# Issuing the three late weight loads of an expert stage one by one

## The reference, cut to what matters

```python
hid = jax.nn.silu(jnp.einsum('nd,edf->nef', t, w_gate)) * jnp.einsum('nd,edf->nef', t, w_up)
hid = hid * combine[:, :, None].astype(hid.dtype)
y = jnp.einsum('nef,efd->nd', hid, w_down)
```

## Time and profile before

| | |
|---|---|
| median of 3 runs | 822.22 us (818.6 to 824.94) |
| the profiled execution's own time | 819.91 us |
| its span in the trace | 818.2 us |
| TensorE busy in the span | 765.6 us, 94% |
| VectorE, ScalarE busy | 605.0 us, 504.0 us |
| HBM read, written | 160.18 MB, 24.12 MB |

### The profile page before, as it was taken

One profiled execution on the slowest core, in us unless ns is written; L12 is line 12 of the kernel. 1 busy time (PEld: TensorE's weight loads), 2 busy tenths in 40 slices (PEclk: granted clock), 3 DMA queues, 4 the chain that ended last, 5 costly groups with the idle time before them and its releaser, 6 DMA issues.

```text
span 818.2 us, 11409 instructions
## 1 busy us (share of the span) xinstructions
PE 765.6 (94%) x4348; PEld 575.1 (70%) x4348; DVE 605.0 (74%) x838; ACT 504.0 (62%) x680; POOL 166.7 (20%) x157
## 2 busy tenths in 40 slices
PE   6999999799999899998998999999999899998993
PEld 4788876464789778777876554657579778876872
DVE  5898994985646798797896467667535789887992
ACT  6778505625315488696884137776735388786892
POOL 5220012400002213332120001043102222332113
PEclk9999999999999999999999999999999899999998
DMA  9975466214834599999987100142073599999953
GB/s 370 239 151 147 86 149 151 37 70 189 304 134 170 219 401 359 320 314 324 325 283 273 70 0 1 52 154 103 1 283 155 211 409 345 326 314 333 314 216 52
DMA packets 35403, 170.91 MB, mean 209 GB/s; under 512 B 7841, under 2 KB 10017, under 8 KB 19728
## 3 DMA queue, kind: packets, MB, share of 16 engines
q1 hardware_dynamic: 18432, 130.03, 41.8%
q0 software_dynamic: 15184, 34.56, 17.8%
q10 hardware_dynamic: 1728, 5.52, 1.9%
HBM read 160.18 MB, written 24.12 MB: 225 GB/s over the span
## 4 chain that ended last, share of the span: by engine, by line
PE 52%; DMA 18%; DVE 17%; ACT 7%; issue 2%; DVEq 1%; ACTq 0%; POOLq 0%; SPq 0%; POOL 0%
DMA ring<-stream 17%; PE PS L2188 9%; DVE w_lo L1117 8%; PE PS L2441 7%; PE PS L1925 7%; PE PS L2319 6%; PE PS L2344 3%; ACT w_hi L754 3%; PE PS L1976 3%; PE PS L2218 2%; PE PS L2476 2%; PE PS L2135 2%; PE PS L2499 1%; DMA arena<-rows 1%; DVE arena L1123 1%
## 5 line engine op out<-in xcount | busy, mean ns | idle before, releaser
L1117 DVE TENSOR_TENSOR w_lo<-ring,w_hi 128x2048 fp32r<-128x2048 f32 x92 | 209.9, 2288 | 42.3 <-ACT w_hi L754 36.1
L754 ACT ACTIVATE w_hi<-ring 128x2048 fp32r<-128x2048 f32 x86 | 164.6, 1916 | 44.0 <-DMA ring<-stream 39.9
L2319 PE MATMUL PS<-w_hi,left_hi 128*128 128x512 f32 x512 | 173.1, 404 | 7.5 <-DVE w_lo L1117 6.8
L2319 PEld LDWEIGHTS PS<-w_hi,left_hi 128*128 128x128 f32 x512 | 96.4, 189 | 30.2 <-issue 6.0
L2319 PE MATMUL PS<-w_lo,left_hi 128*128 128x512 f32 x256 | 99.0, 395 | 0.0
L2344 PE MATMUL PS<-w_hi,left_lo 128*128 128x512 f32 x256 | 85.0, 392 | 7.5 <-DVE left_lo L1117 5.5
L2441 PE MATMUL PS<-ring,hT 128*128 128x512 f32 (+1 forms) x192 | 73.5, 527 | 0.3 <-DVE hT L1117 0.3
L602 POOL DMA_INDIRECT arena<-rows x32 | 41.6, 1299 | 123.8 <-PE PS L2291 110.2
L2344 PEld LDWEIGHTS PS<-w_hi,left_lo 128*128 128x128 f32 x256 | 48.1, 188 | 19.4 <-DVE left_lo L1117 7.2
L2441 PEld LDWEIGHTS PS<-ring,hT 128*128 128x128 f32 x192 | 34.7, 190 | 28.8 <-issue 26.9
L2319 PEld LDWEIGHTS PS<-w_lo,left_hi 128*128 128x128 f32 x256 | 48.9, 191 | 8.6
(11 more groups left out here) (301 smaller groups left out, 1471.2 us busy)
## 6 DMA issues: line engine op xcount, KB each, us to landing
ring<-stream SPq DMA_DIRECT2D x110, 1024.0 KB, 15.9
arena<-stream SPq DMA_DIRECT2D x6, 1024.0 KB, 9.0
ring_split<-stream POOLq DMA_DIRECT2D x11, 512.0 KB, 5.5
rows<-arena POOLq DMA_DIRECT2D x8, 512.0 KB, 3.0
x<-stream SPq DMA_DIRECT2D x4, 1024.0 KB, 6.5
x<-x_in SPq DMA_DIRECT2D x4, 512.0 KB, 5.2
ring_split<-stream POOLq DMA_DIRECT2D x2, 1024.0 KB, 9.0
left_lo<-hT_hi POOLq DMA_DIRECT2D x2, 1024.0 KB, 11.5
```

What stands on the lines that cost most here:

```text
L754: act.activation(w_hi[pair], held_slot(layer, m), ACT.Copy).then_inc(w_hi_done, 1)
L1117: return V.tensor_tensor(out, a, b, op)
L2319: ins = mm(PS[:, gate_bank(e), :], a, b, start=k == 0 and t == 0, stop=k == KD - 1 and t == 2)
```

## The change

The three outside loads that were issued together ahead of ring piece 6 are issued one by one, each ahead of the ring piece that lies eleven pieces before it: 25 ahead of 14, 34 ahead of 23, 43 ahead of 32. The waits for the memory under them stay ahead of piece 6. Since they all count up one semaphore, each load now first waits until the outside loads before it have landed, and ScalarE's copy of an outside piece waits for the landing of that piece, not for all five (7 waits for the first two, like 16).

```diff
@@ -465,7 +465,9 @@
                         sp.wait_ge(first_row_in, 16 * (layer + 1))
                         for n in (NE * layer, NE * layer + 1):
                             sp.wait_ge(got_row[n % 3], fetched(n))
-                        for n in (2, 3, 4):
+                    for n in (2, 3, 4):
+                        if i == EXP0[layer] + AHEAD[n] - 11:
+                            sp.wait_ge(late_in, 16 * (len(AHEAD) * layer + n))
                             load_late(n, layer)
                 if i == QKV0 + 2:
                     sp.wait_ge(zeroed, 2)
@@ -741,7 +743,7 @@
 
                 i, pair = EXP0[layer] + m, expert_pair(layer, m)
                 if m in AHEAD:
-                    act.wait_ge(late_in, 16 * len(AHEAD) * (layer + 1))
+                    act.wait_ge(late_in, 16 * (len(AHEAD) * layer + max(AHEAD.index(m), 1) + 1))
                 else:
                     full, turn = filled(i)
                     act.wait_ge(full, 16 * turn)
```

## The result

The changed kernel is slower: 828.4 us in the median of 6 runs against 822.9 of the kernel before, ratio 1.0083 with an interval of 1.0056 to 1.0111. So the change costs 5.5 us by the medians and 6.8 by the ratio, within the 1% that I had forecast and on the side that I had, but 1.6 to 2 times my 3.4.

The account below looks back on a forecast made before the run. The DMA engines were taken as the bound in the expert stages, TensorE a close second. New holes of 0.7 and 2.7 us, together 3.4, gave 823.3 us from the profiled run or 825.6 from the median; forecast 824.5, range 816 to 832.

Parts of the forecast that it names:

- The DMA sets the stage, and a load costs its work wherever it lies: Expert stages: DMA engines bound, 11.2 us per expert against TensorE's 9.3; moving loads keeps the work, 2.5 us per piece.
- Shorter waits for the first pieces buy nothing: Stage start: pieces 6, 8, 9 land up to 7.5 us earlier; at most 0.9 us gained, left out of the sum.
- None of the outside pieces comes late: Copies of 25, 34, 43: loads issued about 57 or at least 34 us earlier, so idle time there was held impossible.
- TensorE fuller from 345 to 385 us, emptier after: Layer 0: sign expected in the profile, TensorE fuller from 345 to 385 us and emptier from 385 to 411.
- The last awaited piece, 41, sets the end: Layer 0: the busy half's work up to piece 41, landing at 411.5 us, sets the end, so holes are paid in full.
- The holes: Start of each expert stage: new DMA idle time without the burst, 0.7 us in layer 0, 2.7 in layer 1, together 3.4.
- The gathers as cover: Hole count at the stage start: each gather fills 1.25 us of the busy half, three of them 3.75 us.
- The dates: Hole count: issue dates of ring pieces and gathers from the profile before, piece 10 at 288.66 and 660.28 us.
- Rival A: Slower: the ring alone can't keep the DMA busy, holes from 9 us up; up to 15 us, typical 834; chance 0.14.
- Rival B: Faster: an outside load beside the ring fills dry engines, share to 0.99, some 10 us, 812; chance 0.12 with other gains.
- The Trainium skill's rule: Issue early, compute, wait late: speaks against the change, six loads lose their cover; the sum would be the upper bound, 15.0 us.

Follow-up runs that it names:

- e7: Kernel before, burst ahead of piece 6, with the three outside pieces loaded once more at the changed kernel's places: ratio 1.0206 to the kernel before.
- e9: Kernel before without the loads of outside pieces 25, 34 and 43, computing with what lies in their buffers: ratio 0.9867 to the kernel before.
- e5: Changed kernel with all three loads together ahead of piece 10, ScalarE's copies of 7 and 16 waiting for the first two loads alone: 1.0006 to the kernel before.
- e4: Changed kernel with all three outside loads together ahead of piece 10, ScalarE again waiting for all five: ratio 0.9991 to the kernel before.
- e10: The changed kernel measured once more, unaltered, on another chip: ratio 1.0092 to the kernel before, 5.5 us by the medians.
- e6: Changed kernel with all three outside loads together ahead of piece 14, so the early hole stays but nothing is spread: ratio 1.0041 to the kernel before.
- e12: Changed kernel with 32 in place of 20 idle-time transposes on TensorE right before each expert stage: ratio 1.0046 to the kernel before.
- e8: Changed kernel with TensorE's idle time filled by transposes ahead of its waits for pieces 22 to 24 and 31 to 33: ratio 1.0111 to the kernel before.
- e1: The change in layer 0 alone, layer 1's three loads together ahead of piece 6 as before: ratio 1.0035 to the kernel before.
- e2: The change in layer 1 alone, layer 0's three loads together ahead of piece 6 as before: ratio 1.0026 to the kernel before.

## Why the prediction was right in kind and half in size

- **The DMA sets the stage, and a load costs its work wherever it lies**: right. e7 prices a load at 2.8 us, and e9 fits; I had 2.5 from the earlier trace rows. e5's equal time to piece 33 shows the same from the other side.
- **Shorter waits for the first pieces buy nothing**: right. Piece 6 is copied without waiting, and e4 and e5, which keep that and close the hole, are at 0.9991 and 1.0006.
- **None of the outside pieces comes late**: right; the waits of 4 us are those of ring pieces behind them.
- **TensorE fuller from 345 to 385 us, emptier after**: right in layer 0, where it is busy 37.3 us in place of 35.6 and then, to 411 us, 21.7 in place of 25.3. But the two don't cancel, as the hole's loss is in them.
- **The last awaited piece, 41, sets the end**: imprecise. From the copy of piece 33 to that of 47 it takes 42.9 and 42.5 us before and 41.8 and 42.3 after, near 14 times TensorE's 3.1. The end hangs on when piece 33 or so comes, then on TensorE.
- **The holes**: the term that was mis-sized, 0.7 and 2.7 us against 5.4 and 5.0 in the first profile, 2.8 and 3.2 in the second. Two things are in it.
  - *The gathers as cover.* I let each of them fill 1.25 us, 3.75 ahead of piece 10. Counting the same holes, up to piece 13, with the real dates and no gather at all gives 6.8 and 6.2 for the change's profile, 4.3 and 4.7 for e10, 5.8 and 6.0 for e6, 4.0 and 4.2 for e12. What was lost by 33 is less by 1.2 to 1.5 us in these eight stages, by 1.4 and 1.1 in e8, and by 0.9 and 0.5 in the changed stages of e1 and e2. So gathers cover 0.5 to 1.5 us; that is a remainder of the count, and what else may be in it wasn't measured by itself. The reading beneath it, that one half of the engines is the only one that counts, isn't borne out: at 289 us the share of 0.48 is that of one busy half, the rows moved at 99 GB/s, and the time is lost all the same; at 290, at 0.27, the busy half would have had to rest too. Which engines they were no view names. With the dates of before the same count gives holes of 5.7 and 6.5 us without gathers, so with a cover of 1.5 my sum would have come to 4.2 and 5.0; 9.2 in all would have been high, by the 5.5 to 6.8 us measured, and it still lets a piece take 2.5 us.
  - *The dates.* I took the rows' dates as fixed. In the first profile after, TensorE's clock fell at both starts and put piece 10 off by 2 us, and the loss is larger by about as much than in e10 (by 2.6 and 1.8 us). Before, the burst hid it in layer 1. There my rows had the late date in them, and in layer 0 they had not. So my 2.7 for layer 1 lies near e10's 3.2 by luck: a date 2 us too late for that profile and a cover 2 us too long cancel.
  So the range held, but the sum under it was right in its sign and not in its parts.
- **Rival A** (the burst's cover is lost, from 9 us of holes on) was the right mechanism, and its point is reached in one profile and not in the other: the sum of the losses by 33 is 10.4 us and 6.0, against 5.5 to 6.8 timed. Its reason, that a lone load takes longer than its 2.5 us, wasn't tested by itself.
- **Rival B**, that dry engines get filled by a load in flight beside the ring, fails: the share from 345 us on is 0.92, and e7 has loads in flight both ways and 0.92 too.
- **The Trainium skill's rule** to issue early and wait late (DMA: Bandwidth & Descriptors, Rules for kernel authors): its direction agrees with the runs. The page's reason, that the fixed setup cost overlaps, isn't what they show: also after the change each load is issued eleven pieces ahead of its use, and what is lost is work of the DMA in the meantime. Ahead of 6 and ahead of 10 are equally good (e4), and ahead of 14 is not (e6).

## What to carry to other kernels

When transfers are the bound, ask of each date at which one is issued what else the DMA has to do then: a prefetch burst that looks like a queue in front of urgent pieces may be the only work in a stretch in which compute holds the buffers. Moving it behind the urgent pieces is free as long as it still comes before that stretch. And a burst of this kind also covers what varies from run to run, such as a slow start of the compute engine; a sum made with the dates of one profile doesn't see that.

## What the runs showed of the hardware that I had not expected

TensorE at half clock for 3.4 us at the start of a stage goes with about 2 us more of loss by piece 33 where the DMA's queue runs empty (4.3 to 5.7 us against 2.5 to 3.2), and with at most 0.4 us where it is full (107.6 against 107.2 us before; -0.1 to 0.2 us of loss in e4 and e5). In the first profile after it follows waits of 2.0 and 2.55 us for the gathered rows, but a wait of 1.86 us in layer 0 of e1 and one of 2.45 us in layer 1 of e10 weren't followed by it, so the wait alone doesn't decide. In the middle of the stages the half clock came in several runs after waits of over 4 us, and having it once in place of three times bought nothing back (e8 against e10).

Token rows alone keep the DMA's engines busy for a third of the time or more and move little: from 289 to 291 us of the first profile after, 0.21 MB at a mean share of 0.37, about 100 GB/s, where the fullest stretch moves 419 at a share of 1.01.
